# Moving 192 modulation products from VectorE to GpSimd and ScalarE in a two-block transformer kernel

## What is computed

```
c_act = jax.nn.silu(c)
mod = c_act @ w_mod[l] + b_mod[l]
sh1, sc1, g1, sh2, sc2, g2 = [m[:, None, :] for m in jnp.split(mod, 6, axis=-1)]
h = rmsnorm_2(x, attn_norm_g[l]) * (1.0 + sc1) + sh1
...
x = x + g1 * jnp.einsum('bsm,md->bsd', mix, w_out[l])
h = rmsnorm_2(x, mlp_norm_g[l]) * (1.0 + sc2) + sh2
u = jax.nn.relu(jnp.einsum('bsd,df->bsf', h, w_ff1[l]))
x = x + g2 * jnp.einsum('bsf,fd->bsd', u * u, w_ff2[l])
```

## Time and profile before

| | us |
|---|---|
| runs | 2250.6, 2251.22, 2253.33 (median 2251.22) |
| the profiled execution | 2253.74 |
| its span, first to last instruction | 2252.0 |
| TensorE busy in it | 2229.8 (99%) |
| VectorE busy | 1846.3 (82%) |
| ScalarE busy | 1166.8 (52%) |
| GpSimd busy | 111.3 (5%) |
| fused products L1775 on VectorE, 192 | 233.5 |

### The profile page before, as it was taken

The page is one execution under the profiler, slowest core; times in us unless marked ns, Lnnn a source line. Parts: engine busy times, 40 slices in busy tenths (PEclk is TensorE's granted clock), DMA queues, the critical chain, the costliest instruction groups (busy, mean ns, idle before and its releaser), DMA issues.

```text
span 2252.0 us, 34334 instructions
## 1 busy us (share of the span) xinstructions
PE 2229.8 (99%) x12802; PEld 1967.7 (87%) x12802; DVE 1846.3 (82%) x2873; ACT 1166.8 (52%) x1709; POOL 111.3 (5%) x211
## 2 busy tenths in 40 slices
PE   8999999999999999999999999999999999999998
PEld 7888889888888888888898899989988888888887
DVE  7887989889889898998889878998766666666666
ACT  6554665565445454454446568656744434444344
POOL 0000000000111111111110000000000000000000
PEclk9999999999999999999999999999999999999999
DMA  8556664568888888888875564556645555555553
GB/s 318 187 181 248 235 220 154 187 247 290 306 296 297 309 290 319 291 306 291 303 262 186 200 220 145 187 194 224 244 173 197 191 187 190 189 200 187 188 198 119
DMA packets 86883, 515.61 MB, mean 229 GB/s; under 512 B 9781, under 2 KB 10341, under 8 KB 37584
## 3 DMA queue, kind: packets, MB, share of 16 engines
q1 hardware_dynamic: 57168, 405.82, 49.9%
q0 software_dynamic: 28992, 106.43, 14.0%
q10 hardware_dynamic: 576, 1.31, 0.2%
HBM read 511.39 MB, written 2.14 MB: 228 GB/s over the span
## 4 chain that ended last, share of the span: by engine, by line
PE 90%; DVE 6%; ACT 1%; DMA 1%; issue 1%; SPq 0%; ACTq 0%; POOLq 0%; DVEq 0%
PE ps L584 22%; PE ps L598 11%; PE ps L658 8%; PE ps L907 8%; PE ps L908 8%; PE ps L906 8%; PE ps L663 4%; PE ps L654 3%; PE ps L655 3%; PE ps L656 3%; DVE wl L1667 2%; PE ps L690 1%; PE ps L691 1%; PE ps L692 1%; DVE modraw L1775 1%
## 5 line engine op out<-in xcount | busy, mean ns | idle before, releaser
L1667 DVE TENSOR_TENSOR wl<-raw,wh 128x1024 fp32r<-128x1024 f32 x762 | 929.0, 1221 | 298.2 <-ACT wh L1105 296.2
L1105 ACT ACTIVATE wh<-raw 128x1024 fp32r<-128x1024 f32 x766 | 805.2, 1055 | 629.9 <-PE ps L908 309.2
L584 PE MATMUL ps<-xs,wh 128*128 128x512 f32 x1744 | 417.1, 390 | 0.0
L584 PEld LDWEIGHTS ps<-xs,wh 128*128 128x128 f32 x1744 | 322.6, 188 | 63.9
L1775 DVE CUSTOM_DVE_ANT_0 modraw<-modraw,cb 128x1024 f32<-128x1024 f32 x192 | 233.5, 1220 | 22.0 <-DMA modraw<-in_wmod 21.9
L598 PE MATMUL ps<-xs,wl 128*128 128x256 f32 x1744 | 227.1, 283 | 0.0
L598 PEld LDWEIGHTS ps<-xs,wl 128*128 128x128 f32 x1744 | 221.9, 191 | 5.9
L658 PE MATMUL ps<-xs,wh 128*128 128x512 f32 x880 | 223.5, 396 | 1.0 <-issue 1.0
L658 PEld LDWEIGHTS ps<-xs,wh 128*128 128x128 f32 x880 | 158.3, 189 | 30.8 <-issue 1.8
L584 PE MATMUL ps<-xc,wh 128*128 128x512 f32 x608 | 150.2, 389 | 0.0
L534 POOL DMA_DIRECT2D modraw<-in_wmod x172 | 90.8, 528 | 1043.0 <-DVE modp L1775 1039.1
(11 more groups left out here) (368 smaller groups left out, 3550.7 us busy)
## 6 DMA issues: line engine op xcount, KB each, us to landing
raw<-in_w SPq DMA_DIRECT2D x381, 1024.0 KB, 5.1
modraw<-in_wmod POOLq DMA_DIRECT2D x192, 512.0 KB, 4.8
x<-in_x SPq DMA_DIRECT2D x4, 512.0 KB, 8.6
raw<-in_w SPq DMA_DIRECT2D x4, 512.0 KB, 8.9
tbias<-rel_rows POOLq DMA_DIRECT2D x4, 512.0 KB, 6.6
cb<-c_silu POOLq DMA_DIRECT2D x1, 1024.0 KB, 4.9
g2row<-g_rows POOLq DMA_DIRECT2D x1, 1024.0 KB, 10.3
finrow<-in_fin POOLq DMA_DIRECT2D x1, 1024.0 KB, 5.0
```

The lines of the kernel that those rows point to most:

```text
L584: m = nc.tensor.matmul(PS[(b + bi) % 4][:, :], hi[:, t * P:(t + 1) * P], src[k].rearrange("p a t -> p (a t)"), start=opens and first and n ...
L1105: nc.scalar.activation(wh[:, h % HS, :], raw[:, u % RAW, (h % 2) * 1024:(h % 2 + 1) * 1024], ACT.Copy).then_inc(s_round, 1)
L1667: nc.vector.tensor_tensor(wl[:, h % HS, :], raw[:, (h // 2) % RAW, (h % 2) * 1024:(h % 2 + 1) * 1024], wh[:, h % HS, :].bitcast(F32), ALU. ...
```

## The change

VectorE's `mods` and all its calls are gone, and with them the numbers that placed products. In their place:
- GpSimd multiplies each piece with `cb` in place (`multiply`), and signals a new semaphore, `mod_multiplied`. In its queue follow the wait for the copy of the product before (`mod_used`), the load of the next piece into the other slot, and the next multiplication.
- ScalarE sums each product with a copy whose accumulator goes to `modp` (`sum_product`), once at the end of each `step`, from unit 21 on (the condition counts the finished units), until 192 are done. The two embedding units and the five latent units that are not written with `step` get none.

```diff
+        MOD_FROM = U_A + MOD_UNIT
...
-            with pool.Fori(0, POOL_MODS // MOD_SLOTS - 1) as i:
-                for n in range(MOD_SLOTS):
-
-                    pool.wait_ge(s_modu, i * MOD_SLOTS + n + 1)
-                    pool.dma_start(modraw[:, n:n + 1, :],
...
+            def multiply(n, loaded):
+
+                pool.wait_ge(s_modl[n], loaded)
+                nc.gpsimd.tensor_tensor(modraw[:, n, :], modraw[:, n, :], cb[:, 1024 * n:1024 * (n + 1)], ALU.mult
+                                        ).then_inc(s_modx, 1)
...
+            multiply(0, 16)
+            with pool.Fori(0, LOOPED) as i:
+                for n in (1, 0):
+
+                    multiply(n, i * 16 + (16 if n else 32))
+                    pool.wait_ge(s_modu, i * 2 + (1 if n else 2))
+                    pool.dma_start(modraw[:, 1 - n:2 - n, :],
...
+                sum_product()
+
+            def sum_product():
+
+                m = c.n["m"]
+                if c.n["h"] // 2 > MOD_FROM and m < NMOD:
+                    act.wait_ge(s_modx, m + 1)
+                    nc.scalar.activation(modraw[:, m % 2, :], modraw[:, m % 2, :], ACT.Copy, accum_out=modp[:, m:m + 1]
+                                         ).then_inc(s_modu, 1)
+                    c.n["m"] += 1
...
-            def mods(n):
-
-                for j in range(n):
-                    m = c.n["m"]
-                    dve.wait_ge(s_modl[m % 2], 16 * (m // 2 + 1))
-                    nc.vector.tensor_tensor_reduce(out=modraw[:, m % 2, :], in0=modraw[:, m % 2, :],
...
-                gates(CH, first=lambda: product(CH - 1), lo_first=lambda: (h_lo(hs, CH - 1), next_taps()),
-                      mod=lambda j: mods(1 + (j == 4)))
-                token_downs(chunk, lambda: gate_in(CH - 1), lambda: conv(CH - 1), lambda j: mods(1 + (j == 4)))
-                units(CH, product, first=last_sums(chunk), h_lo_of=lambda j: h_lo(hs, j), mod=lambda j: mods(1 + (j in (1, 5))))
+                gates(CH, first=lambda: product(CH - 1), lo_first=lambda: (h_lo(hs, CH - 1), next_taps()))
+                token_downs(chunk, lambda: gate_in(CH - 1), lambda: conv(CH - 1))
+                units(CH, product, first=last_sums(chunk), h_lo_of=lambda j: h_lo(hs, j))
```

More of the change, by code:

```diff
@@ L529, in _, with next_product @@
             pool.dma_start(cb[:, :], bass.AP(tensor=c_dram.tensor, offset=0, ap=[[0, P], [1, KB * P]])).then_inc(s_cb, 16)
[L530 to L541 removed]
+            def multiply(n, loaded):
+                pool.wait_ge(s_modl[n], loaded)
+                nc.gpsimd.tensor_tensor(modraw[:, n, :], modraw[:, n, :], cb[:, 1024 * n:1024 * (n + 1)], ALU.mult
+                                        ).then_inc(s_modx, 1)
+            def next_product(m):
+                multiply(m % 2, 16 * (m // 2 + 1))
+                pool.wait_ge(s_modu, m)
+                pool.dma_start(modraw[:, (m + 1) % 2, :], a["wmod"][m + 1, :, :]).then_inc(s_modl[(m + 1) % 2], 16)
+            LOOPED = 87
+            pool.wait_ge(s_cb, 16)
+            multiply(0, 16)
[4 more added lines that the diff above has]
+                    pool.dma_start(modraw[:, 1 - n:2 - n, :],
+                                   a["wmod"][bass.ds(i * 2 + (2 if n else 3), 1), :, :].rearrange("a p n -> p a n")
+                                   ).then_inc(s_modl[1 - n], 16)
+            next_product(2 * LOOPED + 1)
             pool.wait_ge(s_xs, XS["p"] + 2)
@@ L545, in _ @@
             pool.dma_start(oneh[:, :], a["oneh"]).then_inc(s_rl, 16)
-            mod_loads(POOL_MODS, POOL_MODS + MOD_SLOTS)
+            for m in range(2 * LOOPED + 2, NMOD - 1):
+                next_product(m)
+            multiply((NMOD - 1) % 2, 16 * (NMOD // 2))
             pool.wait_ge(s_rr, 1)
@@ L1085, in _ @@
         def _(act):
[L1086 removed]
+            c, SCALED_OF = Counts(act, m=0, h=0, b=0, t=0, g=0, y=0, k=0, a=0, u=0), []
             def rnd(h):
@@ L2200, in h_lo, with gates @@
                 c.n["l"] += 1
-            def gates(n, first=None, lo_first=None, mod=lambda j: mods(1), rooted=None):
+            def gates(n, first=None, lo_first=None, rooted=None):
                 def late():
@@ L2215, in gates, with units @@
                         half((lambda: gate_in(j - 1)) if j else first, after=(lambda: conv(j - 1)) if j else lo_first)
-                    half(after=lambda: mod(j))
-            def units(n, ev, first=None, lo_first=None, h_lo_of=None, mod=None, last=None, each=lambda i: None):
+                    half()
+            def units(n, ev, first=None, lo_first=None, h_lo_of=None, last=None, each=lambda i: None):
                 for j in range(n):
@@ L2223, in units @@
                                         last() if last and j == n - 1 else None, each(2 * j)))
-                    half(after=lambda: (mod(j) if mod else None, each(2 * j + 1)))
-            def downs(first, lo_first=None, gate=None, mod=None, each=None):
-                for i in range(KB):
-                    half((lambda: add_blocks([i - 1], gate)) if i else first,
-                         after=lo_first if i == 0 else (lambda: each(i)) if each else
-                         ((lambda: mod(i // 2)) if mod and i % 2 else None))
+                    half(after=lambda: each(2 * j + 1))
             def lo_p():
@@ L2250, in sum_take, with token_downs @@
                 m.then_inc(s_evac, 1)
-            def token_downs(chunk, first, lo_first, mod):
+            def token_downs(chunk, first, lo_first):
                 for i in range(2 * CH):
```

40 lines of the change are left out of this document (10 added, 30 removed).

## The result

The changed kernel takes 2454.76 us (median of 4 runs, 2450.28 to 2467.8), the kernel before 2252.04 beside it (4 runs, 2250.6 to 2253.33). The ratio is 1.0905, with a 95% interval of 1.0884 to 1.0927. Predicted were 2477 us and a ratio of 1.10, with 2366 to 2668 as the range. The profiled execution took 2456.24 us, its span 2454.6.

What follows compares the result with a forecast made beforehand. Bound before: TensorE's pace, VectorE close behind; after: GpSimd's serial load and multiplication, period 7.0 us. Added 24 + 183 + 19 = 226 us on 2253.7 gives 2480, median of runs 2477; range 2366 to 2668.

Steps and rivals of the forecast that it cites:

- The period: In units with a product: one load to landing, one GpSimd multiplication and handoffs in series, 7.0 us.
- Landing: Load issue to landing in GpSimd's queue, interpolated between two medians by traffic: 3.9 us.
- Multiplication: GpSimd's product of one piece, taken as fetching its two operands in turn: 2.44 us, lower end 1.22.
- Handoffs: Waking and issuing together in GpSimd's queue, taken once per period: 0.65 us.
- First feed-forward: Units 69 to 196, 128 units growing from 5.57 to 7.00 us: 183 us added.
- Units 22 to 68: 47 units growing from 6.48 to 7.00 us: 24 us added.
- Units 199 to 214: 16 units growing from 5.81 to 7.00 us: 19 us added.
- The relief of VectorE: 250 us of work leave VectorE; only 6 to 34 us count, and nothing where units are paced by the product.
- ScalarE's copies: One copy with accumulator per unit, 1.24 us; ScalarE at 3.96 of 5.57 us, so the work itself is hidden.
- Rival A: GpSimd multiplies as fast as VectorE, period 5.0 us, under the unit's 5.57: faster, 2236 us; chance 0.08.
- Rival B: GpSimd and VectorE hold each other up, 0.6 us per multiplication: period 7.6 us, 2593 us; chance 0.22.
- Rival C: TensorE's clock falls to 1.2 GHz in the long stage: 691 us added, 2942 us; sign: granted clock under 1; chance 0.03.

Runs made afterwards that it cites:

- the run with fills: Changed kernel's order, with GpSimd's multiplication replaced by two multiplications of 2 columns and two constant fills of 1022 columns: 2429.14 us.
- load-ahead: Changed kernel with GpSimd's next load issued before the present multiplication instead of behind it: 2470.24 us, ratio 1.0968.
- the other phase: load-ahead with ScalarE's sum of the product moved by half a unit, behind the first half's rounding quarter: 2498.51 us, ratio 1.1085.
- the rows of the copy: load-ahead with GpSimd multiplying 2 columns and copying 1022 from cb, one wide input instead of two: 2289.63 us.
- four pieces: load-ahead with each whole product done in four GpSimd multiplications of 256 columns: 2562.22 us.

## Why the prediction was right, and where its terms were off

**The direction and the limit** were right: GpSimd's queue can't overlap a load with a multiplication, so the period is their sum, and the units with a product grow. Each of the 128 multiplications waited for a load, and the run with fills shows the same period with VectorE not held up.

**The period** came out at 6.77 us, not 7.0. Landing: 3.9 predicted, 3.98 measured. The interpolation between the two medians came out well, but there is luck in it: it took the landing to depend on the traffic alone. From 500 to 1150 us the median landing is 3.8 us in the changed kernel, 4.5 with load-ahead and 5.4 in the other phase, all at 230 to 233 GB/s. Multiplication: 2.44 predicted by two passes; 2.345 is the shortest, 2.35 to 2.41 the undisturbed one, 2.74 the mean, since in this kernel GpSimd waits for VectorE as well (up to 3.41). The Trainium skill, GPSIMD Engine Reference, Performance versus the Vector engine, led to an estimate of 2.25; the undisturbed rows are 4 to 7% above it. Handoffs: 0.65 predicted, 0.06 measured. This is the term that was mis-sized. 702.33 to 702.98 in the earlier trace rows was the time from VectorE's release to a DMA that had waited for it; a multiplication that waits for its load starts 0.08 us after the landing, and the next load's issue follows the multiplication with no gap. Errors of +0.1 and +0.3 in two terms and -0.6 in the third left -0.2: the period came out nearer than its terms were.

**The stretches.** First feed-forward: +183 predicted and +149 measured; 128 x 0.27, the error of the period over 6.73, is the whole difference. Units 22 to 68: +24 predicted, +23 measured. Units 199 to 214: +19 and +21. Yet these two are right in size only by accident. In the run with the chain and without the hold-up of VectorE, units 22 to 68 take 6.69 us each, +10 on the old length, and units 199 to 214 take 6.48, +11; the other 13 and 11 us come with the hold-up, which the forecast had left out.

**The relief of VectorE** was put at 6 to 34 us if the units were not paced. It is 4.4 alone, and nothing with ScalarE's copies added (2254.32). The earlier trace rows had said so: TensorE waited 2.5 us in all for VectorE. I took the 34 from the chain's shares, which name the engine that a step ran on, not the time that its removal would give. Rival A, at 2236, was too good by 12 us or more.

**ScalarE's copies** as hidden work: right. With 1.05 + 0.19 us per unit more and no chain or hold-up, the kernel takes 2254 us.

**Rival B** was described rightly and priced too simply. It put 0.6 us on each multiplication for a wait behind VectorE; measured are 0.35 (2.74 in the mean against some 2.4), and in the measured period they are offset by the handoffs, which the forecast had put too high. The other direction, VectorE behind GpSimd, had no price: up to 2.7 us per meeting. The chain and the hold-up are not added up: each alone costs about the same (176 us and 219 us), and both together 203. While the chain paces the units VectorE has 1.2 us more per unit to lose, and in the first feed-forward all of the hold-up vanishes in that; that this room is the reason is argued, not shown by a run of its own. The Trainium skill, SBUF — State Buffer, Who interferes with whom, says that the pair contends when VectorE has two SBUF inputs and GpSimd reads SBUF, not when GpSimd only writes, and not when VectorE has at most one SBUF input. By the rows of the copy (yf 1.22), of the fills (hg 0.43) and of tk (0.42) the trace agrees on all three. It says too that the order of issue decides which one blocks; hg, which by the trace began 0.40 us before the multiplication and needed 0.43, was nevertheless held until 0.29 us after it, and there the measurement differs.

**Rival C**, the clock, came true in a small way. It fell to the lower of its two levels several times and came back each time: 0.98 in the mean over the 862 us of the first feed-forward is some 34 us at half speed. No time was lost by that in the long stretch as far as the runs show, for the run with fills has 0.96 there and the same period. So the sign that the prediction gave for C was seen, and its price of 691 us was not. One fall, about 1334 us, behind a gap in TensorE's work:

```profile
1330.00:1332.00 2.00, 1.41 (x11) 1.13 (x9) 2.00 (x3) 0.97 (x2) 1.54 (x2) 1.00 0.65 250
1332.00:1334.00 2.00, 0.00 (x0) 0.00 (x0) 1.97 (x4) 1.40 (x4) 0.00 (x0) 1.00 0.99 414
1334.00:1336.00 2.00, 0.00 (x0) 0.00 (x0) 1.97 (x4) 1.10 (x2) 0.85 (x1) 0.51 0.24 94
```

**What stays open**: why four pieces, run one after the other, leave hg and up no turn while subtractions get one; what besides the traffic sets the landing of a load; and how far a place could be found in the unit where the multiplication meets no instruction with two SBUF inputs at all. Two places were tried, both inside the loop.

No kernel here beats the one before by more than 0.2%, and none that computes the result does at all. The 4 us of the relief are the most that could be had, and only with the work done by nobody.

## What to carry to other kernels

Write down the queue of the engine that gets the work, and ask which of its waits can overlap: a load issued behind the instruction that frees it makes load plus compute the period, however many buffers there are. Before moving work off an engine, ask whether TensorE waits for that engine at all; here it did for 2.5 us of 713. And when a cure changes nothing, look in its trace for the next cause before giving up the first: two limits of the same height hide each other, and only the run without either shows it. Ask, too, of a term that came out right whether its cause did: here two stretches had the predicted size, half of it from a hold-up that the sum had not contained.

## What the runs showed of the hardware

- A GpSimd multiplication of two 128x1024 fp32 tiles takes 2.35 to 2.41 us undisturbed, 1.30 for 512 columns, 2.82 in four pieces of 256; a copy of 1022 columns 1.04, a constant fill 0.95.
- Beside it, VectorE's instructions with both inputs in SBUF end 0.28 to 0.29 us (256 columns) or 1.08 to 1.09 us (1024 columns) after GpSimd has finished, whether they began before or after it: 0.43 us become 3.1, 1.22 become 3.8. Those with an input from PSUM keep their length (0.42, 0.68), and so do all beside a fill or a DMA's issue.
- GpSimd waits for VectorE as well: the multiplication takes 2.74 us in the mean and up to 3.41 beside VectorE's subtractions.
- Four GpSimd instructions in a row (2.82 us) hold hg or up for all four. Subtractions that were under way take turns with them: 5.03 us for the four and 4.57 for three subtractions.
- The landing of a 512 KB load is not set by the traffic alone. In the changed kernel's order it grows with it (3.98 us in the mean at 6.77 us per unit, 4.52 at 6.16, 4.91 at 5.68), but at the same 230 to 233 GB/s the median is 3.8, 4.5 or 5.4 us, depending on the order of GpSimd's queue and the place of the sum.
- GpSimd's multiplication starts 0.08 us after the landing that it waits for.
